# A two-block transformer kernel: another order of loads, chunk 0 in halves, keys ahead of values with heads 0 and 1 scored amid the last values, and the output in four parts

## What is computed

```
xn = rms_norm(x, norm_mix[0])
q, k, v = split(xn @ w_qkv)            # 1024 x 3072, 8 heads of 128
q, k = partial_rope(q), partial_rope(k)
s = where(key <= query, q @ k.T / sqrt(128), -inf)   # 256 tokens: one own block
x = x + (softmax(s) @ v) @ w_o
x = x + squared_relu_mlp(rms_norm(x, norm_mlp[0]))   # up 1024 x 4096, down
```

## Time and profile before

| | |
|---|---|
| median of 3 runs | 1194.12 us |
| the profiled execution | 1193.4 us |
| its span, first to last instruction | 1191.6 us |
| mean granted TensorE clock | 0.984 |
| busy: PE, PE's weight loads, DVE, ACT, POOL | 1132.8, 1008.9, 677.9, 531.0, 41.9 us |
| read from HBM, written | 194.73 MB, 1.05 MB |

### The profile page before, as it was taken

How to read it: one execution, slowest core, us unless ns; L and a number is a source line. 1 busy time by engine, 2 the same in 40 slices (tenths; PEclk the granted TensorE clock), 3 DMA queues, 4 the chain that set the end, 5 groups by cost and what they waited for, 6 DMA issues and landing times.

```text
span 1191.6 us, 17784 instructions
## 1 busy us (share of the span) xinstructions
PE 1132.8 (95%) x7114; PEld 1008.9 (85%) x7114; DVE 677.9 (57%) x936; ACT 531.0 (45%) x644; POOL 41.9 (4%) x69
## 2 busy tenths in 40 slices
PE   4999999999999999997899999999999989999997
PEld 3887799999889999976767999999798768999996
DVE  4745644544664454466635655554765767555554
ACT  4446443443444344345434544334543664443342
POOL 0000000000000000000000000000410310000000
PEclk9999999999999999998979999999999998999999
DMA  9752446556534655544512466556754242556550
GB/s 351 254 179 69 143 157 210 166 187 202 186 104 156 206 170 187 189 128 159 177 36 71 141 188 198 177 176 224 223 177 156 86 134 72 188 177 199 176 176 35
DMA packets 127450, 196.36 MB, mean 165 GB/s; under 512 B 7393, under 2 KB 97633, under 8 KB 127281
## 3 DMA queue, kind: packets, MB, share of 16 engines
q1 hardware_dynamic: 124256, 186.29, 47.5%
q0 software_dynamic: 3152, 9.51, 2.7%
HBM read 194.73 MB, written 1.05 MB: 164 GB/s over the span
## 4 chain that ended last, share of the span: by engine, by line
PE 84%; DVE 9%; ACT 4%; issue 1%; DMA 1%; DVEq 0%; SPq 0%; ACTq 0%
PE ps L1395 26%; PE ps L1397 26%; PE ps L1396 26%; DVE wlo L895 2%; ACT whi L596 1%; DVE xs L1001 1%; ACT junk L627 1%; DMA raw<-attn_w_qkv_in 1%; PE ps L1501 1%; PE ps L1787 1%; PE ps L1785 1%; DVE act_lo L1015 1%; PE ps L1417 1%; DVE x L1046 1%; DVE xs L1042 1%
## 5 line engine op out<-in xcount | busy, mean ns | idle before, releaser
L895 DVE TENSOR_TENSOR wlo<-raw,whi 128x2048 fp32r<-128x2048 f32 (+2 forms) x173 | 389.1, 2266 | 178.9 <-ACT whi L596 177.8
L1395 PE MATMUL ps<-act_hi,whi 128*128 128x256 f32 x1384 | 392.7, 284 | 6.4 <-DVE act_lo L1015 3.4
L1396 PE MATMUL ps<-act_lo,whi 128*128 128x256 f32 x1384 | 391.7, 283 | 0.0
L1397 PE MATMUL ps<-act_hi,wlo 128*128 128x256 f32 x1384 | 391.6, 283 | 0.0
L596 ACT ACTIVATE whi<-raw 128x2048 fp32r<-128x2048 f32 (+2 forms) x172 | 321.2, 1888 | 114.1 <-PE ps L1397 99.4
L1395 PEld LDWEIGHTS ps<-act_hi,whi 128*128 128x128 f32 x1384 | 263.5, 190 | 11.3 <-issue 8.3
L1396 PEld LDWEIGHTS ps<-act_lo,whi 128*128 128x128 f32 x1384 | 263.6, 190 | 2.0
L1397 PEld LDWEIGHTS ps<-act_hi,wlo 128*128 128x128 f32 x1384 | 263.6, 190 | 0.0
L1397 PE MATMUL ps<-whi,hlo 128*128 128x512 f32 x400 | 156.8, 392 | 0.0
L1396 PE MATMUL ps<-wlo,hhi 128*128 128x512 f32 x400 | 156.8, 392 | 0.0
L1395 PE MATMUL ps<-whi,hhi 128*128 128x512 f32 x400 | 156.2, 390 | 0.0
(11 more groups left out here) (157 smaller groups left out, 889.8 us busy)
## 6 DMA issues: line engine op xcount, KB each, us to landing
raw<-mlp_w_up_in SPq DMA_DIRECT2D x32, 1024.0 KB, 6.4
raw<-mlp_w_down_in SPq DMA_DIRECT2D x32, 1024.0 KB, 4.9
raw<-ffn_w_gate_in SPq DMA_DIRECT2D x22, 1024.0 KB, 5.3
raw<-ffn_w_up_in SPq DMA_DIRECT2D x22, 1024.0 KB, 5.4
raw<-ffn_w_down_in SPq DMA_DIRECT2D x22, 1024.0 KB, 4.8
raw<-attn_w_qkv_in SPq DMA_DIRECT2D x12, 1024.0 KB, 8.6
raw<-w_kv_shared_in SPq DMA_DIRECT2D x8, 1024.0 KB, 7.0
raw<-attn_w_o_in SPq DMA_DIRECT2D x4, 1024.0 KB, 4.9
```

The costliest lines, as they stand in the source:

```text
L895: nc.vector.tensor_tensor(wlo[:, s, 0:width], raw[:, s, 0:width], whi[:, s, 0:width].bitcast(F32), ALU.subtract).then_inc(lo_ready, 1)
L1395: nc.tensor.matmul(dst, lhsT=left[0], rhs=right[0], start=start, stop=False, **kw)
L1396: nc.tensor.matmul(dst, lhsT=left[0], rhs=right[1], start=False, stop=False, **kw)
L1397: return nc.tensor.matmul(dst, lhsT=left[1], rhs=right[0], start=False, stop=stop, **kw)
```

## The change

- SP loads the constants first, then x, then chunk 0 in two halves with a semaphore each, then chunk 1 and the others. The row for mix0 goes out from ACT's queue, the positions from POOL's, and POOL's other rows wait until `hi_ready` is 2.
- ACT and DVE take chunk 0 half by half, between quarters 1 and 2 of the turned x; PE uses its halves in the same order. PE has eight small matmuls on the identity ahead of the first turning.
- The six column groups of QKV are taken in the order 0, 2, 1, 3, 4, 5. The last turning of heads and the second half (kh = 1) of the last values' products move into the attention's loop, at h = 2, behind the scores of heads 0 and 1. The `keep_busy` calls of this attention are gone.
- The first up product of an MLP goes to bank 5, and the second doesn't wait for `act_done`.
- The output is stored in four parts; `lo_before(AT["bwo"] + 3)` becomes `+ 2`.

The diff, cut to its core:

```diff
...
+        QKV_ORDER = (0, 2, 1, 3, 4, 5)
...
             if kind == "qkv":
-                return w_qkv[i % 2, i // 2]
+                return w_qkv[i % 2, QKV_ORDER[i // 2]]
...
-            def first_row():
-                sp.dma_start(rows[:, 0, :], row_source["mix0"].partition_broadcast(P)
-                             .rearrange("q a n -> q (a n)")).then_inc(first_row_loaded, 16)
-
+            sp.dma_start(const[:, 0:C_CAUSAL], a["const"][:, 0:C_CAUSAL]).then_inc(const_loaded, 16)
             sp.dma_start(x[:, :, :], a["x"][0].rearrange("(t p) n -> p t n", p=P)).then_inc(x_loaded, 16)
-            first_row()
-            sp.dma_start(const[:, 0:C_CAUSAL], a["const"][:, 0:C_CAUSAL]).then_inc(const_loaded, 16)
-            load_one(0)
+            first = source("qkv", 0)
+            for h, landed in enumerate((first_half_loaded, w_loaded[SLOT[0]])):
+                sp.dma_start(raw[:, SLOT[0], h * D:(h + 1) * D].rearrange("p (k f) -> p k f", f=HALF),
+                             first[:, 2 * h:2 * h + 2]).then_inc(landed, 16)
             load_one(1)
-            for n, name in enumerate(("positions", "positions_2")):
-                sp.dma_start(pos_i[:, n, :], a[name].rearrange("a (t p) -> p (a t)", p=P),
-                             allow_slow_non_contiguous=True).then_inc(pos_loaded, 16)
             for c in range(2, AT["mlp0"]):
...
             for t in range(TT):
-                sp.wait_ge(x_ready, 4 * 9 + 2 * (t + 1))
-                sp.dma_start(out[0, t * P:(t + 1) * P, :], x[:, t, :]).then_inc(out_stored, 16)
-            sp.wait_ge(out_stored, 16 * TT)
+                for h in range(2):
+                    sp.wait_ge(x_ready, 4 * 9 + 2 * t + h + 1)
+                    cols = slice(h * HALF, (h + 1) * HALF)
+                    sp.dma_start(out[0, t * P:(t + 1) * P, cols], x[:, t, cols]).then_inc(out_stored, 16)
+            sp.wait_ge(out_stored, 16 * 2 * TT)
...
+            for n, name in enumerate(("positions", "positions_2")):
+                pool.dma_start(pos_i[:, n, :], a[name].rearrange("a (t p) -> p (a t)", p=P),
+                               allow_slow_non_contiguous=True).then_inc(pos_loaded, 16)
+            pool.wait_ge(hi_ready, 2)
             for name in ROWS[1:ROW["pre1"] + 1]:
...
-            def attention(at, w_o):
+            def attention(at, w_o, fill):
                 for h in range(at.heads + 3):
+                    fill(h)
                     g = h - 2
                     if 0 <= g < at.heads:
                         copy_probs(at, g)
...
-                    nc.scalar.activation(relu, bank(4), ACT.Relu).then_inc(f.act_done, 1)
+                    nc.scalar.activation(relu, bank(5 if first else 4), ACT.Relu).then_inc(f.act_done, 1)
...
-            hi_next()
-            copy_turned("mix0")
+            act.dma_start(rows[:, 0, :], row_source["mix0"].partition_broadcast(P)
+                          .rearrange("q a n -> q (a n)")).then_inc(first_row_loaded, 16)
+            copy_turned("mix0", (0, 1))
+            for h, landed in enumerate((first_half_loaded, w_loaded[SLOT[0]])):
+                act.wait_ge(landed, 16)
+                nc.scalar.activation(whi[:, SLOT[0], h * D:(h + 1) * D], raw[:, SLOT[0], h * D:(h + 1) * D],
+                                     ACT.Copy).then_inc(hi_ready if h else first_half_hi, 1)
+            cursor[0] = 1
+            copy_turned("mix0", (2, 3))
             hi_before(0)
             stats("mix0")
...
-            for n in range(6):
-                hi_before(2 * n + 1)
-                act.wait_ge(w_used, 2 * n + 2)
+            def copy_qkv(i):
+                n = QKV_ORDER[i]
+                hi_before(2 * i + 1)
+                act.wait_ge(w_used, 2 * i + 2)
                 dst = qk_tok[:, 0, n * HALF:(n + 1) * HALF] if n < 4 else V[:, 0, (n - 4) * HALF:(n - 3) * HALF]
-                nc.scalar.activation(dst, bank(2 * (n % 2)), ACT.Copy, scale=norm_stat("mix0", 0, 6))\
+                nc.scalar.activation(dst, bank(2 * (i % 2)), ACT.Copy, scale=norm_stat("mix0", 0, 6))\
                     .then_inc(qkv_a, 1)
-                if n >= 3:
-                    copy_heads(act, n - 3)
-            copy_heads(act, 3)
-            attention(moba, AT["wo"])
+
+            for i in range(5):
+                copy_qkv(i)
+                if i >= 3:
+                    copy_heads(act, i - 3)
+            copy_heads(act, 2)
+            hi_before(10)
+
+            def last_values(h):
+                if h == 2:
+                    copy_heads(act, 3)
+                    copy_qkv(5)
+
+            attention(moba, AT["wo"], last_values)
             hi_before(AT["wo"] + 2)
             copy_turned("mlp0")
...
-            def attention(at, masks, w_o):
+            def attention(at, masks, w_o, fill):
                 for h in range(at.heads + 4):
+                    fill(h)
                     if h < at.heads:
                         mask = masks(h)
                         dve.wait_ge(at.scored, h + 1)
...
-            lo_next()
-            split_turned("mix0")
+            split_turned("mix0", (0, 1))
+            for h, done in enumerate((first_half_lo, lo_ready)):
+                dve.wait_ge(hi_ready if h else first_half_hi, 1)
+                cols = slice(h * D, (h + 1) * D)
+                nc.vector.tensor_tensor(wlo[:, SLOT[0], cols], raw[:, SLOT[0], cols],
+                                        whi[:, SLOT[0], cols].bitcast(F32), ALU.subtract).then_inc(done, 1)
+            cursor[0] = 1
+            split_turned("mix0", (2, 3))
             lo_before(0)
...
-            for n in range(6):
-                lo_before(2 * n + 1)
-                dve.wait_ge(w_used, 2 * n + 2)
+            def copy_qkv(i):
+                n = QKV_ORDER[i]
+                lo_before(2 * i + 1)
+                dve.wait_ge(w_used, 2 * i + 2)
                 dst = qk_tok[:, 1, n * HALF:(n + 1) * HALF] if n < 4 else V[:, 1, (n - 4) * HALF:(n - 3) * HALF]
-                nc.vector.tensor_scalar(dst, bank(2 * (n % 2) + 1), norm_stat("mix0", 1, 6), None, ALU.mult)\
+                nc.vector.tensor_scalar(dst, bank(2 * (i % 2) + 1), norm_stat("mix0", 1, 6), None, ALU.mult)\
...
                 if n < 4:
-                    dve.wait_ge(qkv_v, n + 1)
-                    dve.wait_ge(qkv_a, n + 1)
+                    dve.wait_ge(qkv_v, i + 1)
+                    dve.wait_ge(qkv_a, i + 1)
...
+
+            for i in range(5):
+                copy_qkv(i)
+            lo_before(10)
+
+            def last_values(h):
+                if h == 3:
+                    copy_qkv(5)
+
             dve.wait_ge(masks_loaded, 16)
-            attention(moba, lambda h: (causal[:, P:T], causal), AT["wo"])
+            attention(moba, lambda h: (causal[:, P:T], causal), AT["wo"], last_values)
...
-            lo_before(AT["bwo"] + 3)
+            lo_before(AT["bwo"] + 2)
...
-                    moba: (0, 0, 2, 7), mla: (0, 0, 2, 1)}
+                    moba: (0, 0, 0, 0), mla: (0, 0, 2, 1)}
...
                     pe.wait_ge(const_loaded, 16)
+                    for _ in range(8):
+                        nc.tensor.matmul(bank(7, 0, P), lhsT=ident, rhs=ident, start=True, stop=True)
...
-            def attention(at, score, value, w_o, final):
+            def attention(at, score, value, w_o, final, fill):
                 for h in range(at.heads + 3):
-                    if h == 2 and at is moba:
-                        qkv_done()
+                    fill(h)
                     if h < at.heads:
                         if h >= 2:
                             pe.wait_ge(at.maxed, h - 1)
...
-                def up(c, i, value, first=False):
+                def up(c, i, value, first=False, second=False):
                     wait_chunk(value)
-                    if not first:
+                    if not first and not second:
                         pe.wait_ge(f.act_done, i)
-                    tiles_out(slot(c), 4, norm if first else None).then_inc(w_used, 1)
+                    tiles_out(slot(c), 5 if first else 4, norm if first else None).then_inc(w_used, 1)
...
-                up(n0 + 1, 1, n0 + 2)
+                up(n0 + 1, 1, n0 + 2, second=True)
...
-            for n in range(6):
-                for kh in range(2):
-                    c = 2 * n + kh
-                    wait_chunk(c + 1)
-                    if n >= 2 and kh == 0:
-                        pe.wait_ge(qkv_a, n - 1)
-                        pe.wait_ge(qkv_v, n - 1)
-                    if n == 0:
-                        wait_acts("mix0", 2 * kh + 2)
-                    for t in range(TT):
-                        for k in range(4):
-                            ins = product(bank(2 * (n % 2) + t), acts(4 * kh + k, t * P, (t + 1) * P),
-                                          cols(slot(c), k * HALF, (k + 1) * HALF),
-                                          start=kh == 0 and k == 0, stop=kh == 1 and k == 3)
+            def qkv_products(i, kh):
```

(48 more changed lines are left out.)

50 lines of the change are left out of this document (25 added, 25 removed).

## The result

The changed kernel took **1185.57 us** (median of four; 1177.27 to 1187.12) beside 1195.06 for the kernel before on the same chip; the ratio of the runs is **0.9907** (95% interval 0.9887 to 0.9928), which on the 1194.12 shown is 1183.0. I had said 1187.7, 1184.0 to 1191.5: faster, rightly, but by 6.4 us where it is 11, and outside my range. A later comparison of the two gave 0.992 (0.990 to 0.9939).

What follows compares the result with a forecast made beforehand. TensorE was taken as the bound, 1132.8 of 1191.6 us; start -6.05, attention +2.25, MLPs -1.87 and output -0.4 sum to -6.1 us, from 1193.8 (halfway between profiled execution and median) to 1187.7, range 1184.0 to 1191.5.

Steps and rivals of the forecast that it cites:

- The start: Loading x and chunk 0: first product at 13.3 instead of 19.35, 6.05 us gained; ends 3.65 and 7.0.
- the 1.6 us that I had named as an upside: First products: half of 3.3 us lost at the 1.2 GHz pace can come back; start then capped at about 7.
- rival B: Start held by chunk 3 landing at 23.5 again: start gives 3.65, sum -3.7, time 1190.1; chance 0.15.
- Attention: First attention up to w_o: -0.5 + 0.85 + 1.9, 2.25 us lost; ends 0.5 gained, 7.25 lost.
- The chain of three waits: First attention: three waits in a row replace the one removed, 18.8 us against 19.3, only 0.5 gained.
- +0.85: First attention: at 1.2 GHz, PE's steps on the chain double, costing 0.85 us.
- half of 3.8 is 1.9: w_o's first products run at half pace until the clock is back, costing 1.9 us.
- my main case: Whole kernel, clock falling in attention: sum -6.1 us, 1187.7, by itself 1185.5 to 1190; chance 0.61.
- rival A: The clock holds in the first attention: sum -8.8 us, time 1185.0; chance 0.15.
- Rival C: Low clock stays through attention's heads, 27.6 us at half pace: 5.8 us slower, 1199.6; chance 0.04.
- The MLPs: Idle time ahead of the second up product goes: 0.93 us twice, 1.87 gained; ends 1.5 and 1.9.
- the output: End of kernel: last issue carries 256 KB instead of 512, 0.4 us gained; 0 to 0.75.

Runs made afterwards that it cites:

- e14: The kernel of e8 with the start of the kernel before: 1179.39 us against e8's 1173.69.
- e1: The changed kernel run again, nothing altered: 1185.5 us over six executions, 0.992 of the kernel before.
- e10: The kernel of e8 with chunk 0 in one transfer and its high and low parts made whole: 1177.52 us (0.9855).
- e15: The kernel of e5 with the attention's part of the change added: 1188.14 us (0.9943).
- e16: The kernel of e6 with the attention of the kernel before: 1177.32 us (0.9854).
- e7: The changed kernel with the copies of the last turned heads and last values put ahead of chunk 15's parts: 1179.58 us (0.9885).
- e8: The changed kernel with both e7's moved copies and e6's filler matmuls: 1173.69 us (0.9826), the fastest.
- e11: The kernel of e6 with six more constant matmuls behind chunk 11 in the first attention: 1180.0 us (0.9877).
- e3: The kernel before with only the change's QKV order and first attention: 1193.17 us (0.9979), five of twelve executions at 1186.7 to 1187.1.
- e6: The changed kernel with three constant matmuls in each 1.47 us TensorE gap of the second block's first attention: 1178.72 us (0.9871).
- e5: The kernel before with three constant matmuls in each 1.47 us TensorE gap of the second block's first attention: 1189.01 us (0.9952).
- e18: The kernel before, unchanged, traced again to meet a longer execution: 1196.42 us.
- e4: The kernel before with only bank 5 for the first up product and the four-part output: 1191.48 us (0.9956), four of twelve at 1183.5 to 1184.0.
- e2: The kernel before with only the start of the change: 1189.58 us (0.9962), five executions.
- e13: The kernel of e8 with ten constant matmuls in the 5.6 us gap of the second block's low-rank part: 1175.03 us (0.9828).

## Why the prediction was wrong, point by point

**The start** was forecast at 6.05 and is 5.7 by e14 (5.4 by the means), 5.3 in the change's trace. That it is so near is luck: two errors nearly cancel. I let x land at 7.9 by counting the bytes asked for ahead of it, as if the loads behind it would wait; it was scaled from 9.88, and in later traces of the same start from anywhere between 8.8 and 10.5. Against that the first products ran at full pace in the change's trace, the 1.6 us that I had named as an upside, as in four of the ten others with the small matmuls. Chunk 3 came by 20.55 against the 21.0 that I asked for, so rival B falls (e1 has 21.09). The Trainium skill's page "DMA: Bandwidth & Descriptors" (Queues, rings and completion order) has the engines take turns between queues, from which I had estimated 20.4; the landing agrees with the estimate, but no row here shows the shares. Halving chunk 0 is worth more than its 1.1 us of my working (e10).

**Attention** was forecast at +2.25 and is about +0.3 (e15, e16), +1.3 in the change's own trace. The chain of three waits stood as written: PE resumed at 3.2 us behind chunk 11's end, 3.15 forecast, and e7 and e8 show that ACT's place at chunk 15 was its cause. With the low clock gone before w_o, the new order gains 0.1 to 0.4 us, against the -0.5 of my sum (0.3, had I read 19.05 for 19.3). **The step that failed is the price of the clock in this term, "+0.85" and "half of 3.8 is 1.9", 2.75 us in my main case.** The pace of the scores is hidden (e11), and the clock was back at w_o's second matmul in the change's trace and before w_o in those of e3, e6 and e15; a second stretch of it ahead of w_o, in the traces of the change and e1, costs 1.4 to 1.9 us against the others. So between my case and rival A, nearer A. Rival C's persistence through the heads was met in none of the traces.

**The MLPs** brought 1.0 a layer in the trace (0.93 forecast), **the output** about 0.6 (0.4 forecast). The Trainium skill's page "DMA: Bandwidth & Descriptors" (Anatomy of one DMA) fits 2.0 us and the bytes at 436 GB/s to transfers issued from GpSimd, while these go out from SP's queue. Its fit would have a part of 256 KB land after 2.6 us, where the trace has 2.1, and the whole of 512 KB after 3.2, where it had 2.6; the difference of 0.6 that it gives for halving is close to the 0.5 measured.

**The sum** by the priced terms is then -5.7 + 0.3 - 2.0 - 0.6 = -8.0, where I had -6.1, and the attention's term makes all of the difference (1.95). From 1193.4, the traced execution whose rows I used, to 1186.3, the mean of eight of ten, are 7.1 us. But from e5 to e6, both traced without the spell near 593 us and neither with a short kind, are 9.7, and 1.7 of these are in no term: in the two traces it is the start, at full pace there and worth 6.8.

**The second step that failed** stands in one sentence: the forecast was made "from halfway between" the profiled execution and the median, as if each kernel had one time. The mean of the kernel before is 1194.7, 1.3 above its profiled execution, because two in five of its executions are longer by 2.6 us (in e18's trace, by longer stretches of low clock). The mean of the changed kernel is 1184.7, 1.6 below its typical one, because two in ten are 8 us shorter, as far as their clocks tell without the spell near 593 us. Together 1.3 + 7.1 + 1.6 = 10.0, which is what the means of all executions show; this is how the 10.0 divides, not a proof of its cause, and the 9.7 from e5 to e6 warn that the spell is not all of it. I had the row that should have warned me: the earlier trace rows show a clock that fell behind 7.05 of 10 us of work, and I took it as a fixed cost of the kernel, priced it into the attention and never asked what would happen if, after the shift of 6 us, it didn't fall where it had fallen.

What stays open: why the spell was in all 54 executions of the kernel before, by their times, and missing in some of the change, of e3 and of e4; e2, with the start alone, had it in all five, by their times too. Whether the new start also took the longer low spell at the start away is open too; e2's executions lie within 1.5 us, but no trace pair shows it. And some 1.3 of e10's 3.5 to 3.8 us are in no trace.

## What to carry over

Before moving transfers or work among engines, write down which instructions stand in each engine's own order ahead of the one that the critical engine waits for: one line's move (a copy ahead of a chunk's high part) was worth 5 us here, about half of what the whole change brought. Take several executions of both kernels before believing a difference of a few us, look whether their times fall into groups, and compare group with group. A low-clock spell behind short gaps is not a fixed cost of the kernel; in the gaps of 1.47 us here, three spare matmuls each kept it away.

## What the runs showed of the hardware that I had not expected

- The same work (7.05 of 10 us busy, two gaps of 1.47 us) was followed by a granted clock of 0.54 over 15 us in the traces of the kernel before and of the change, and of 1.00 in e4's: 6.2 us of span in the traces, 7 to 8 us between the kinds of executions. Filling both gaps held it in the traces of all eleven kernels that had them filled.
- Filling 4.5 of a gap of 5.6 us (e13) did not: the clock fell behind it to 0.57.
- A row of the granted clock may say 1.00 while matmuls of 512 columns last 0.77 us and follow at the half pace, as at 19.35 in the earlier trace rows; there the durations are the surer sign:
```profile
19.30:22.70 3.40, 3.35 (x8) 1.00 1.05 387
```
- In the twelve traces with the new order of loads, DVE could begin on x (1 MB, with the row of gains landed before it) at between 8.8 and 10.5 us.
